# MLP up projections: tokens stationary, 512 weight columns moving, and 16 block transposes per panel on VectorE

## The reference, cut to what matters

```python
D_MODEL = 2048; SEQ = 256; DEPTH = 2; D_FF = 4 * D_MODEL
for i in range(DEPTH):
    ...
    x = layer_norm(ALPHA * x + y, ln1_g[i], ln1_b[i])
    ff = jnp.square(jax.nn.relu(x @ mlp_w1[i])) @ mlp_w2[i]
    x = layer_norm(ALPHA * x + ff, ln2_g[i], ln2_b[i])
```

## Time and profile before

| what | value |
|---|---|
| median of three runs | 2341.82 us (2341.13 to 2342.14) |
| the profiled execution | 2341.61 us, of which 2339.9 us is the span |
| TensorE busy | 2323.7 us, 99% of the span, 14594 matmuls |
| weight loads busy | 2021.9 us, 86% |
| VectorE busy | 1419.7 us, 61% |
| ScalarE busy | 1057.9 us, 45% |
| GpSimd busy | 247.3 us, 11% |
| the 32 up panels' matmuls | L659 646.2 us and L662 402.4 us, 2048 of each |
| the chain that ended last | TensorE 96%, VectorE 1%, issue 1%, ScalarE 1% |

### The profile page before, as it was taken

The page is one execution under the profiler, slowest core; times in us unless marked ns, Lnnn a source line. Parts: engine busy times, 40 slices in busy tenths (PEclk is TensorE's granted clock), DMA queues, the critical chain, the costliest instruction groups (busy, mean ns, idle before and its releaser), DMA issues.

```text
span 2339.9 us, 37244 instructions
## 1 busy us (share of the span) xinstructions
PE 2323.7 (99%) x14594; PEld 2021.9 (86%) x14600; DVE 1419.7 (61%) x1528; ACT 1057.9 (45%) x1363; POOL 247.3 (11%) x254
## 2 busy tenths in 40 slices
PE   9999999999999999999999999999999999999999
PEld 8898888888888888888989899888888888888887
DVE  5664667555555555568666767566755655555557
ACT  5455454434434434435545445445443443443442
POOL 0152001001000000000032322200100100000000
PEclk9999999999999999999999999999999999999999
DMA  7663456665666666665534435354666566567664
GB/s 254 181 176 122 149 196 199 201 192 181 200 192 184 196 192 188 193 210 155 172 118 145 127 113 159 109 196 145 199 198 193 181 200 192 181 198 229 185 196 137
DMA packets 237771, 417.25 MB, mean 178 GB/s; under 512 B 23825, under 2 KB 47146, under 8 KB 236330
## 3 DMA queue, kind: packets, MB, share of 16 engines
q1 hardware_dynamic: 236250, 412.82, 56.4%
q10 hardware_dynamic: 1360, 2.10, 0.2%
HBM read 412.77 MB, written 2.10 MB: 177 GB/s over the span
## 4 chain that ended last, share of the span: by engine, by line
PE 96%; DVE 1%; issue 1%; ACT 1%; DMA 0%; POOL 0%; ACTq 0%; POOLq 0%; DVEq 0%
PE quad L659 20%; PE quad L684 14%; PE quad L685 14%; PE quad L686 14%; PE quad L662 10%; PE quad L630 5%; PE quad L632 5%; PE quad L634 5%; PE quad L739 1%; PE quad L1177 1%; PE quad L860 1%; PE quad L934 1%; PE quad L932 1%; PE quad L933 1%; PE quad L889 1%
## 5 line engine op out<-in xcount | busy, mean ns | idle before, releaser
L1755 DVE TENSOR_TENSOR wlo<-raw,whi 128x1024 fp32r<-128x1024 f32 x760 | 984.8, 1303 | 702.4 <-ACT whi L1328 699.7
L1328 ACT ACTIVATE whi<-raw 128x1024 fp32r<-128x1024 f32 x760 | 800.9, 1058 | 885.6 <-PE quad L686 464.8
L659 PE MATMUL quad<-xs,whi 128*128 128x512 f32 x2048 | 646.2, 396 | 1.7 <-issue 1.2
L684 PE MATMUL quad<-whi,hh 128*128 128x512 f32 x1248 | 488.8, 392 | 1.0 <-POOL hl L2430 1.0
L686 PE MATMUL quad<-whi,hl 128*128 128x512 f32 x1248 | 485.9, 389 | 0.0
L685 PE MATMUL quad<-wlo,hh 128*128 128x512 f32 x1248 | 485.6, 389 | 0.0
L662 PEld LDWEIGHTS quad<-xs,wlo 128*128 128x128 f32 x2048 | 384.7, 188 | 90.5
L662 PE MATMUL quad<-xs,wlo 128*128 128x256 f32 x2048 | 402.4, 278 | 0.0
L659 PEld LDWEIGHTS quad<-xs,whi 128*128 128x128 f32 x2048 | 312.8, 189 | 3.1 <-issue 2.1
L684 PEld LDWEIGHTS quad<-whi,hh 128*128 128x128 f32 x1248 | 234.3, 188 | 49.9 <-POOL hl L2430 1.4
L686 PEld LDWEIGHTS quad<-whi,hl 128*128 128x128 f32 x1248 | 234.2, 188 | 49.3
(11 more groups left out here) (335 smaller groups left out, 2119.6 us busy)
## 6 DMA issues: line engine op xcount, KB each, us to landing
raw<-in_mlp_w SPq DMA_DIRECT2D x512, 512.0 KB
raw<-in_gdn_w_in SPq DMA_DIRECT2D x105, 512.0 KB
raw<-in_w_out SPq DMA_DIRECT2D x64, 512.0 KB
raw<-in_mem_w_kv SPq DMA_DIRECT2D x32, 512.0 KB
raw<-in_mla_w_in SPq DMA_DIRECT2D x25, 512.0 KB
raw<-in_mla_w_ukv SPq DMA_DIRECT2D x24, 256.0 KB
gb<-in_ln_g SPq DMA_DIRECT2D x4, 1024.0 KB, 7.6
gb<-in_ln_b SPq DMA_DIRECT2D x4, 1024.0 KB, 9.7
```

The lines of the kernel that those rows point to most:

```text
L659: last = nc.tensor.matmul(both, b.whi[:, slot, k, cols], b.xs[:, :, kt, :], start=start, stop=stop, skip_group_check=True)
L684: nc.tensor.matmul(ps[:, t, 0:n], ah[:, kt, toks], hi[:, k, 0:n], start=start, stop=False)
L1328: nc.scalar.activation(b.whi[:, c % NSPLIT], b.raw[:, slot], ACT.Copy).then_inc(sem.hi_ready, 1)
L1755: nc.vector.tensor_tensor(b.wlo[:, c % NSPLIT], b.raw[:, c % NRAW], b.whi[:, c % NSPLIT].bitcast(F32), ALU.subtract).then_inc(sem.lo_ready, 1)
```

## The change

Up panels now go through `panel_r`, like the down panels: tokens stationary, 512 weight columns moving. The result stands with tokens on the partitions, in two banks, as one sum per value. At the panel's end ScalarE copies it with relu to `rows` in SBUF and frees the PSUM half. VectorE turns `rows` into `relu` with features on the partitions: 16 transposes, each of 32 partitions, one for every pair of a source quarter and a destination quarter of the partitions, and each with eight blocks of 32x32 (two token halves by four column tiles), so 256 elements per partition. Then VectorE squares `relu` in place. `low` and `panel_up` are gone, and `rows` takes the space of `low`.

```diff
@@ mlp and mlp_group, TensorE
-                    panel_up(p0, c0, after_turn(turned), part=(k, k + 1))
+                    panel_r(p0, c0, PANEL, b.xh, b.xl, after_turn(turned), part=(k, k + 1))
...
-                    panel_up(p0 + u, c0 + u * PANEL, after_turn(turned), off, poff,
-                             part=(done if u == 0 else 0, PANEL))
+                    panel_r(p0 + u, c0 + u * PANEL, PANEL, b.xh, b.xl, after_turn(turned), off=off, poff=poff,
+                            part=(done if u == 0 else 0, PANEL))
@@ mlp_group, ScalarE
                     if m:
-                        act.wait_ge(sem.panel_free, g * 2 * UP + (PANEL_AT[name] + u))
-                    nc.scalar.activation(b.low[:, :, :], quad_ps[(PANEL_AT[name] + u) % 2][:, :, S:2 * S],
-                                         ACT.Copy).then_inc(sem.low_out, 1)
+                        act.wait_ge(sem.rows_free, g * UP + m)
+                    nc.scalar.activation(b.rows[:, :, :], panel_ps[(PANEL_AT[name] + u) % 2], ACT.Relu).then_inc(sem.panel_free, 1)
                     split(c0 + NSPLIT + u * PANEL + PANEL - 1, off)
                     act.wait_ge(sem.sq_done, g * UP + (m + 1))
@@ mlp_group, VectorE
-                        dve.wait_ge(sem.low_out, g * UP + (m + 1))
+                        dve.wait_ge(sem.panel_free, g * 2 * UP + (PANEL_AT[name] + u + 1))
                         if u >= 2:
                             dve.wait_ge(sem.hid_lo, g * UP + (m - 1))
                         s_ = b.relu[:, u % 2, :]
-                        nc.vector.tensor_tensor(s_.rearrange("p (k s) -> p k s", s=S),
-                                                quad_ps[(PANEL_AT[name] + u) % 2][:, :, 0:S], b.low[:, :, :],
-                                                ALU.add).then_inc(sem.panel_free, 1)
-                        dve.wait_ge(sem.panel_free, g * 2 * UP + (PANEL_AT[name] + u + 1))
-                        nc.vector.scalar_tensor_tensor(out=s_, in0=s_, scalar=0.0, in1=s_, op0=ALU.max,
-                                                       op1=ALU.mult).then_inc(sem.sq_done, 1)
+                        turned = s_.rearrange("p (j t c) -> p t j c", j=4, t=TT)
+                        rows = b.rows[:, :, :].rearrange("p t (j c) -> p t j c", j=4)
+                        for i in range(4):
+                            for o in range(4):
+                                src, dst = slice(32 * i, 32 * i + 32), slice(32 * o, 32 * o + 32)
+                                last = nc.vector.transpose(turned[dst, :, :, src], rows[src, :, :, dst])
+                        last.then_inc(sem.rows_free, 1)
+                        dve.wait_ge(sem.rows_free, g * UP + (m + 1))
+                        nc.vector.tensor_tensor(s_, s_, s_, ALU.mult).then_inc(sem.sq_done, 1)
```

More of the change, by code:

```diff
@@ L295, in place @@
     b.diag, o = at("diag", [P, P], F32, o)
-    b.low, o = at("low", [P, 2 * UP // 2, S], F32, o)
+    b.rows, o = at("rows", [P, TT, CN], F32, o)
     return b
@@ L344, in __init__ @@
         self.half_rows = signal("half_rows")
-        self.low_out = signal("low_out")
+        self.rows_free = signal("rows_free")
         self.sq_done = signal("sq_done")
@@ L635, in panel_t @@
                                                     stop=stop, skip_group_check=True)
[L636 to L663, removed]
                     last.then_inc(sem.chunk_used, 1)
```

## The result

| kernel | median | runs | ratio to before (95% interval) |
|---|---|---|---|
| before | 2341.48 us | 2341.02 to 2342.14 | |
| changed | 2460.15 us | 2457.68 to 2460.60 | 1.0505 (1.0491 to 1.0519) |

The change makes the kernel 118.7 us slower; 2443 was forecast, with a range of 2380 to 2510. The kernel before has four runs here, the three named at the start and one more. The profiled execution took 2460.60 us, its span is 2458.9 us.

What follows compares the result with a forecast made beforehand. TensorE, busy 99%, was taken as the bound. New waits of 3.67 us a panel less 0.52 gained make 3.15, times 32 is 101 us on 2341.6: 2443 us, range 2380 to 2510.

Steps and rivals of the forecast that it cites:

- TensorE's gain: Fewer matmuls in up panels: 0.066 us a chunk, 0.52 us a panel, 16.8 us over 32 up panels.
- t: Time from one VectorE transpose's start to the next at an up panel's end: 0.44 us, range 0.40 to 0.52.
- The pair of copies at 0.85 us: Two VectorE copies in the earlier trace, read as going to different partition halves: end to end, 0.425 us each.
- overlap: Rival: transposes overlap like copies on the same rows, 0.32 us from start to start; 2381 us, chance 0.10.
- side by side: Rival: four transposes on different output quarters run at once, 1.7 us for all sixteen; 2325 us, chance 0.04.
- half pace: Rival: float32 goes through the transposer at half pace, 0.69 us a transpose; 2571 us, chance 0.10.
- The slack: Length of transposes behind an up panel's end that stays hidden before TensorE must wait: 3.37 us.
- The first gap: TensorE's new wait ahead of chunk 3 behind an up panel's end: 2.84 us.
- the second: TensorE's new wait ahead of chunk 4 behind an up panel's end: 0.83 us.
- the tighter chunk: Behind an up panel's end, chunk 4 has 2.11 us to spare, chunk 3 has 2.94, though chunk 4 is needed later.
- The sum: Per up panel, 7.04 us of transposes less 3.37 hidden, less 0.52 gained: 3.15 net, times 32 is 101 us.
- the falls of the clock: Rival: TensorE's clock halves for the chunk behind the gap, 1.89 us a panel, +60 us; 2504 us, chance 0.08.

Runs made afterwards that it cites:

- grouped kernel: The changed kernel with its sixteen transposes each within one quarter of the partitions, four in a row per quarter (hidden layer not the reference's): 2399.18 us.
- e1_one: The changed kernel with one block transpose of 128 partitions by 1024 elements in place of the sixteen (hidden layer not the reference's): 2323.37 us.
- filled kernel: The changed kernel with 20 unread TensorE transposes between chunk 2 and the wait for chunk 3 behind each up panel: 2448.43 us.
- e3_act4: The changed kernel with ScalarE writing `whi` of chunk 4 before it waits for the square, not after `hh`: 2443.82 us.
- e6_eight64: The changed kernel with 8 transposes of 64 partitions by 256 elements, halves in turn, for the sixteen (hidden layer not the reference's): 2332.04 us.

## Why the prediction was right, point by point

- **What bounds the kernel.** This was right: with VectorE's price taken away the time fell by TensorE's gain alone, 18 us where 16.8 were worked out.
- **The transposes.** t was put at 0.44 and measured 0.451. The pair of copies at 0.85 us was the row to go by, but the prediction misread it: by the kernel's code the two L2319 copies write the same half of the partitions and read from different halves of PSUM, while most steps of the change alter only what is written. That one price held for both is in part luck; only the runs show it. The grouped kernel shows the rule of the Trainium skill (VectorE: DVE Perf Modes, "Two Vector instructions with no wait between them") at work on transposes: 0.33 to 0.37 us with overlap where the quarter stays, none where it changes. The rivals of overlap and side by side fell by the changed kernel's own rows, where no transpose overlaps another; half pace fell by the 0.451 and by `e1_one`.
- **The slack.** 3.37 us was worked out; the traces show 3.67. Counted from the panel's first matmul, chunk 4 starts at 10.88 us with one transpose, at 12.95 behind 5.74 us of transposes and at 14.43 behind 7.22: both leave 3.67. The first gap was forecast at 2.84 and is 2.73, the second at 0.83 and is 0.64. The forecast counted TensorE's need from weight load to weight load. Before, the load starts 0.23 us ahead of its matmul (600.52 and 600.75); behind a wait the two start together (612.56), so a matmul is that much less late. This explains most of the 0.30 us. That the tighter chunk is chunk 4, for the sake of `hh` and `hl`, was right (`e3_act4`).
- **The sum.** 3.15 us net a panel was forecast, and 25.44 - 22.29 = 3.15 measured. That it fits so well is luck: t was too low by 0.011, which is 0.18 us a panel, the slack was too low by 0.30, and the slow start of chunk 4 behind its wait, 0.13, was not in the sum. That step gives 101 of the 118.7 us.
- **What the sum left out.** First, the falls of the clock: I took them for a rival with a chance of 0.08, all panels or none. They came in 18 of 32 panels and cost 12 us by the filled kernel. The price per panel was too high: 1.89 us forecast, some 0.8 measured for one fall. The forecast let a whole chunk of 2.72 us run at half pace, so 5.44 us; the fall lasts 3.4. Second, the first groups: their residual instructions stand behind the split of chunk 3 and lengthen two panels of each layer by 1.0 us, 4 us in all (26.41 to 26.43 against 25.44 us in the filled kernel); I had not counted them. With the 101 these make 117; the last 2 us I can't place, and the changed kernel's own runs lie 2.9 us apart. Neither term was in the sum, so that 2460 still lies within the range worked out from t alone (2422 to 2483) says little of the mechanism; the gaps and periods above do.
- **Open.** Why the clock falls behind one gap of 2.57 us and not behind the next one of the same length wasn't tested. The falls come to 17 us by counting periods (16 x 0.81 + 2 x 2.07) and to 12 by the filled kernel's median; the two profiled executions differ by 13.4 (2460.60 and 2447.16). Set side by side, their panels show where most of the rest is. Three of the falls stand in first groups, in or next to the panels that are late anyway, and cost 0.07, 0.51 and 0.02 us there. And one stretch of down panels in the filled kernel is 1.5 us longer than the same stretch in other groups, for which I have no cause.

## What to carry to other kernels

A list of short instructions between two steps that feed the critical engine costs its whole length minus the slack, however idle the engine is on average; write down when each later step is wanted, and put the short ones between the steps, not ahead of them. The first is shown by one transpose against sixteen (137 us), the second by the same sixteen in another place (2460.15 against 2325.44 us). The step that is tightest can be a later one, because of what another engine puts in front of it. And when VectorE must move rows between quarters of the partitions, count each instruction at its full duration.

## What was not expected of the hardware

- An idle stretch of TensorE of 2.57 us was enough for the granted clock to go to 0.50 in 18 of 32 cases, for 3.4 us in 16 and for 6.8 us in 2. It fell between 0.7 us before work resumed and 1.3 us after. Stretches of up to 1.5 us in the grouped kernel never did it, nor did the one stretch of 2.25 us, at the start of the kernel with one transpose. 20 transposes on TensorE, 0.11 us apart, in the same gap held the clock at 1.00 in all 32.
- What a block transpose costs goes by the elements per partition, and hardly by the number of partitions: 436 ns for 32x256, 440 ns for 64x256, 1245 ns for 128x1024. If the partitions make no difference in the last one either, an estimate from these is 1.05 ns an element and 0.17 us for the instruction.
- A chunk for which TensorE had waited started slowly: its second matmul came 0.33 to 0.34 us behind its first instead of 0.227, and that was so too in `e6_eight64`, where the split was ready only just in time.
